# The last two layer visits of a two-block transformer kernel: linear heads' output products behind the first scores, pieces of gate and output products behind the transposes

## The reference

```
h = rmsnorm(x); z = h @ w_in              # linear heads q,k,v, gates, low-rank c, rope key
o_gla = rmsnorm(gla_mix(q, k, v, log_a)) * silu(g_gate)       # linear attention, 4 heads, chunks of 64
q = rmsnorm(c_q) @ w_uq;  kv = rmsnorm(c_kv) @ w_ukv;  head norms and rope
o_mla = block_causal_attention(q, k, v) * silu(m_gate)        # 4 softmax heads of 128
x = x + concat([o_gla, o_mla]) @ w_out[l]
```

## Time and profile before

| | us |
|---|---|
| three runs of the kernel | 1118.04, 1120.25, 1122.82 |
| median | 1120.25 |
| the profiled execution | 1117.79 |
| its span, first to last instruction | 1115.9 |
| TensorE busy in the span | 981.8 (88%) |
| VectorE, ScalarE, GpSimd busy | 657.9, 325.7, 526.7 |
| mean granted TensorE clock | 0.963 of full speed |

### The profile page before, as it was taken

How to read it: one execution, slowest core, us unless ns; L and a number is a source line. 1 busy time by engine, 2 the same in 40 slices (tenths; PEclk the granted TensorE clock), 3 DMA queues, 4 the chain that set the end, 5 groups by cost and what they waited for, 6 DMA issues and landing times.

```text
span 1115.9 us, 11288 instructions
## 1 busy us (share of the span) xinstructions
PE 981.8 (88%) x3307; PEld 530.3 (48%) x3307; DVE 657.9 (59%) x1547; ACT 325.7 (29%) x816; POOL 526.7 (47%) x578
## 2 busy tenths in 40 slices
PE   3999999999997787887769989889899987998997
PEld 3858655864543332332325534434453532554653
DVE  5867776885864865865675576477445554242142
ACT  4113322222221211121143625313363430262251
POOL 1210011767777777777667645656564562100000
PEclk9999999999999899899989999989899988999999
DMA  9998855999999999999999999999999998955750
GB/s 343 318 385 328 313 198 176 378 376 406 409 409 411 411 413 412 411 414 408 400 412 408 410 407 406 403 410 398 411 411 407 405 372 316 396 222 170 258 195 19
DMA packets 142042, 394.92 MB, mean 354 GB/s; under 512 B 16745, under 2 KB 23457, under 8 KB 141857
## 3 DMA queue, kind: packets, MB, share of 16 engines
q0 software_dynamic: 75392, 274.86, 62.6%
q1 hardware_dynamic: 64224, 118.61, 29.3%
q10 hardware_dynamic: 2368, 0.76, 0.3%
HBM read 393.15 MB, written 1.05 MB: 353 GB/s over the span
## 4 chain that ended last, share of the span: by engine, by line
PE 55%; DMA 24%; POOL 8%; issue 6%; DVE 4%; ACT 2%; POOLq 0%; SPq 0%; DVEq 0%; ACTq 0%
PE bank L1755 18%; DMA wring<-in_peer_u,ids 14%; PE bank L1803 13%; PE bank L1489 7%; POOL wring L993 5%; DMA R<-in_w_in 4%; DMA wring<-in_ada_w 3%; PE bank L1824 3%; PE bank L1566 2%; DMA wring<-in_peer_v,ids 2%; POOL R L993 2%; PE bank L1479 1%; DVE wring L2367 1%; PE bank L1850 1%; DMA last_row<-in_peer_v,ids 1%
## 5 line engine op out<-in xcount | busy, mean ns | idle before, releaser
L2367 DVE CUSTOM_DVE_ANT_0 wring<-wring,bank 128x1024 f32<-128x1024 f32 x224 | 273.0, 1219 | 223.3 <-DMA wring<-in_peer_u,ids 220.9
L993 POOL DMA_INDIRECT wring<-in_peer_v,ids x224 | 216.3, 966 | 163.9 <-PE bank L1755 73.0
L1755 PE MATMUL bank<-wring,R 128*128 128x512 f32 x496 | 242.7, 634 | 45.8 <-ACT R L1247 32.9
L993 POOL DMA_INDIRECT wring<-in_peer_u,ids x224 | 212.6, 949 | 76.0 <-issue 57.3
L1755 PE MATMUL bank<-wring,modb 128*128 128x512 f32 x384 | 183.8, 619 | 26.3 <-ACT modb L1247 13.4
L1755 PEld LDWEIGHTS bank<-wring,R 128*128 128x128 f32 x496 | 96.8, 202 | 173.1 <-issue 141.7
L1755 PEld LDWEIGHTS bank<-wring,modb 128*128 128x128 f32 x384 | 71.8, 196 | 116.1 <-issue 89.8
L1032 POOL TENSOR_SCALAR small<-small 128x1 f32<-128x1 f32 (+3 forms) x13 | 2.5, 193 | 218.2 <-ACTq L1328 125.1
L1803 PE MATMUL bank<-R,hT 128*128 128x512 f32 (+1 forms) x192 | 90.4, 599 | 7.1 <-DMA R<-in_w_in 7.1
L1803 PE MATMUL bank<-wring,hT 128*128 128x512 f32 (+1 forms) x192 | 86.4, 600 | 4.3 <-ACT hT L1428 2.7
L1489 PE MATMUL bank<-hT,wring 128*128 128x256 f32 x304 | 70.9, 392 | 2.5 <-DVE hT L2050 1.0
(11 more groups left out here) (387 smaller groups left out, 1269.8 us busy)
## 6 DMA issues: line engine op xcount, KB each, us to landing
wring<-in_w_in SPq DMA_DIRECT2D x14, 2048.0 KB, 12.9
wring<-in_ada_w SPq DMA_DIRECT2D x8, 2048.0 KB, 13.7
R<-in_w_in SPq DMA_DIRECT2D x8, 2048.0 KB, 19.6
wring<-in_w_out SPq DMA_DIRECT2D x6, 2048.0 KB, 10.8
wring<-in_ada_w SPq DMA_DIRECT2D x8, 1024.0 KB, 15.3
R<-in_w_out SPq DMA_DIRECT2D x4, 2048.0 KB, 19.7
wring<-in_peer_wq SPq DMA_DIRECT2D x2, 2048.0 KB, 10.2
wring<-in_peer_u,ids POOLq DMA_INDIRECT x224, 12.4
```

The costliest lines, as they stand in the source:

```text
L993: pool.indirect_dma_start(dst, None, table, bass.IndirectOffsetOnAxis(index, 0)).then_inc(landed, 16)
L1755: last = pe.matmul(pb[half][:, :], diag[b][:, s, :], v_place(n, b, s)[:, half * 512:(half + 1) * 512], start=False, stop=last_row, skip_gr ...
L2367: dve.tensor_tensor_reduce(row, row, h_psum(t), 1.0, 0.0, ALU.mult, ALU.add, a8[:, b, s:s + 1]).then_inc(u_free, 1)
```

## The change

Only the list of `tail_schedule()` is another. Everything that is computed stays, with the same instructions.

```
-    out = [("y2", 1, 0, p) for p in range(4)]
+    out = []
...
-            out += [("y2", 1, 1, p) for p in range(4)]
+        ch = v - LAYERS
+        out += [("y2", 1, ch, p) for p in range(3)]
         to(("zT",), ("zTe",))
-        out.append(("y2e", 1, v - LAYERS))
+        out += [("y2", 1, ch, 3), ("y2e", 1, ch)]
...
-        to(("U",), ("st",), ("ms", 0), ("mk", 0), ("mk", 1), ("mx", 0), ("mx", 1), ("ms", 1), ("mk", 2), ("mg", 2), ("mk", 3))
-        to(("mPT", 0), ("mPTe", 0), ("mPT", 1), ("mPTe", 1), ("mx", 2), ("mx", 3), ("go",), ("gosq",), ("rms", 3))
-        to(("mPV", 0), ("mPV", 1), ("mg", 3), ("mge",), ("mPT", 2), ("mPTe", 2), ("mPT", 3), ("mPTe", 3), ("goe",))
-        to(("mPV", 2), ("mPV", 3), ("moe",), ("cT2", 0), ("cT2e", 0))
-        to(*[("y2", ch, p) for ch in range(2) for p in range(2)], ("cT2", 1), ("cT2e", 1))
+        to(("U",), ("st",), ("ms", 0), ("mk", 0), ("mk", 1), ("mx", 0), ("mx", 1), ("go",), ("gosq",), ("rms", 3), ("ms", 1), ("mk", 2), ("mk", 3))
+        to(("mPT", 0), ("mPTe", 0), ("mPT", 1), ("mPTe", 1), ("mx", 2), ("mx", 3), ("goe",), ("mPV", 0), ("mPV", 1))
+        to(("mPT", 2), ("mPTe", 2), ("mPT", 3), ("mPTe", 3), ("mg", 2), ("mPV", 2), ("mPV", 3), ("cT2", 0), ("cT2e", 0))
+        to(("mg", 3), ("mge",), ("moe",), ("y2", 0, 0), ("y2", 0, 1), ("y2", 1, 0), ("cT2", 1), ("cT2e", 1), ("y2", 1, 1))
```

## The result

| | us |
|---|---|
| changed kernel, median of five | 1113.11 (1111.15 to 1113.55) |
| kernel before, median of five | 1120.07 (1118.04 to 1122.82) |
| ratio of the two, 95% interval | 0.9932 (0.9913 to 0.9952) |
| profiled execution of the changed kernel, its span | 1113.40, 1111.6 |

The change makes the kernel 7.0 us faster; 6.1 was predicted. By the interval it is between 5.4 and 9.7. Profile against profile the gain is only 4.4 us (1117.79 to 1113.40), and when both kernels were measured again (the first experiment) their medians were 5.3 us apart. Where the differences lie is the question of the experiments.

A forecast was written before the change was run, and what follows sets the result against it. From 950 us on TensorE's work bounds the kernel, so closing its holes saves time: 2 x 2.6 + 0.8 - 0.7 + 1.7 - 0.85 = 6.1 us, 1120.25 to 1114.1. Its own range was 1111 to 1117; 1110.5 to 1118.5 with two rivals.

The forecast's parts named there:

- Inside a visit: From the first scores' end to the last output piece: 29.43 us becomes 26.8, 2.6 saved per visit, 5.2 for both.
- the linear output: TensorE product moved to the start of the count, ahead of the second scores, priced at 1.84 us without a wait.
- The wait that the change opens: Behind the first transposes TensorE waits for VectorE's masks and copy: 1.7 us per visit, bounds 1.4 to 2.1.
- No slack at the third value product: Copy behind the linear heads allows it at 9.34 us, TensorE arrives at 9.35; without the covering gate piece 1.7 open.
- The starts of the visits: Moving one output piece behind the normed transposes loses 0.7 us in visit 2 and saves 0.8 in visit 3.
- The clock: Visit 2's half-clock stretch goes, 1.7 us gained; a possible new one at its start costs 0.85, between 0 and 1.7.
- the other case: If transposes counted as a busy TensorE for the clock, the summed gain would be nearer 7.0 us than 6.1.
- the old hole of 2.9 us: Mid-visit stretch of waits and one transpose group before the change; the clock fell behind it in visit 2, not 3.
- 3.75 us for four product rows: Rows after an idle 3.50 us, read as some 1.9 above four at full clock, 1.72.
- Half the gain: Rival: copies and the product behind the linear heads come later, 1.3 us lost a visit; gain 3.5, 1116.8 us; chance 0.14.
- the clock eats it: Rival: full-price slow stretch at visit 2's start and one left in a visit; gain 3.6, 1116.6 us; chance 0.14.
- slower: Rival: linear heads reach VectorE too late for a late root, holes over 3 us; +4.1, 1124.4 us; chance 0.06.

The follow-up runs named there:

- the first experiment: The changed kernel measured again against the kernel before, also called the second comparison: 1113.16 us against 1118.48, ratio 0.9946.
- the cover gone: Changed kernel with the moved gate piece taken from ahead of the third value product and set beside the last gate piece: 1116.30 us, ratio 0.9968.
- the starts alone: Kernel before with only the left-open output piece moved behind the normed transposes: median 1123.07 us in twelve runs, ratio 1.0025; once more, 1123.22.
- the inside alone: Changed kernel with all four left-open output pieces ahead of the normed transposes again, keeping only the new order inside visits: 1112.71 us, ratio 0.9949.
- four pieces ahead: Changed kernel with all four left-open output pieces ahead of the transposes in visit 2, three still in visit 3: 1111.31 us, ratio 0.9931.
- the first copies ahead: Changed kernel with the mask of head 3 moved behind the copies of heads 0 and 1: 1111.61 us, ratio 0.9929.

## Why the prediction was right, and where it was off

**Inside a visit: right, 0.2 short.** Predicted 2.6 us, measured 29.43 - 26.99 = 2.44. The term that was off most is the linear output, 2.04 (1083.42 - 1081.38) instead of 1.84; what makes it longer behind the first scores than behind transposes was not tested. Two heads times values take 1.16 instead of 1.09. The wait that the change opens was predicted at 1.7; it is 1.5 to 1.6, since the second scores end at about 1085.5, the transposes take 0.44 and the product starts at 1087.53 (the profile gives it as 1.40 of idle time, with the transposes' end modelled later). The place (the copy behind the last mask) and the release by VectorE are as predicted.

**No slack at the third value product: right.** Predicted 9.34 and 9.35; in the trace the product starts at 1090.87, 9.49 on that count, with the gate piece ending 0.02 before. With the cover gone the hole was 1.74, predicted 1.7.

**The starts of the visits: the waits right, one term 0.2 short.** In visit 2 0.7 is lost, as predicted. In visit 3 the gain is 1.0, not 0.8: from the transposes to the end of `c` before it is 1047.82 - 1039.69 = 8.13 us, after it 1045.95 - 1037.13 = 8.82, of which the moved piece is 1.72. The prediction counted the copy's wait alone; `c` itself also takes 6.23 instead of 6.46 us when it follows another product without a wait (7.95 less the piece's 1.72). So the starts give 0.3 together, as the kernels with one part alone show: the starts alone 0.3 under the kernel before, the inside alone 0.3 over the changed kernel, four pieces ahead 1.0 under the inside alone, all at full clock (152.7, 148.19 and 147.16 us of tail).

**The clock: the places right, the sizes and one premise off.** For the start of visit 2 I took half of 1.7. The full 1.7 was paid in five of the six profiled executions that have the longer wait there (the changed kernel twice, the cover gone, the first copies ahead, the starts alone once of twice), and in none of the six whose wait stayed at 0.6. The rule of the Trainium skill, page "TensorE: Matmul & The Clock Gate", section "Part 4: PE-mode transpose", that a transpose does not count as a busy TensorE, gave the better number for the profiled pair (5.3 against 5.2 measured in the tail); the runs do not show it by themselves, since no kernel had the transposes away. The 7.0 that the prediction had for the other case equals the difference of the medians, but by luck: it puts the price at the start of visit 2 at nothing, and the full 1.7 was paid. For visit 2 I took away 1.7, from one profile; two more profiles of the kernel before show 2.9 and 3.0, and the kernel with the starts alone shows that it can fall in both visits. That the shorter waits of the new order keep the clock up is true mostly, not always: behind the old hole of 2.9 us it fell in five of ten visits, behind the new one, 2.0 us on the same count and 1.40 of it idle, in one of ten (visit 2 with the cover gone; never in the changed kernel's four). These are few cases, and what decides in a single one stays open.

One reading of the prediction is wrong without bearing on the sum: 3.75 us for four product rows is 2.0 above 1.72, not 1.9.

So of the gain 5.2 is from holes (153.05 us of tail at full clock before, 149.56 - 1.7 = 147.9 after; predicted 5.3). What remains of the median's 7.0 is argued and not shown: two of three profiles of before gave back 2.9 to 3.0 in visit 2 where 1.7 is now paid at the start, which makes 6.4, inside the interval of 5.4 to 9.7. The 7.0 is itself partly chance: its median of the kernel before, 1120.07, stands above the 1118.48 and 1118.17 of the later comparisons, and the second comparison gives 5.3 by medians and 6.0 by its ratio. That 6.1 lies between is in part luck: against those two profiles both of its terms for the clock were too small, the 1.7 given back and the 0.85 paid, and the two errors work against each other. How often the clock falls in executions without a profile stays open, and the profiled executions begin their tails up to 3.2 us apart (957.89 to 961.12), for causes that were not followed.

**The rivals.** "Half the gain" and "slower" needed a later copy or a later root; both were on time. Of "the clock eats it" the first half came true, the slow stretch at the start, and not the second, one left in a visit.

## What to carry to other kernels

When every hole of the leading engine has another engine's name, lay out both engines' lists on one time line and put independent work of the right length into each hole, one piece per hole; a piece that stands where the engine waits for something else anyway (the start of visit 2) costs nothing there, and taking it away cost 0.7 us of waiting and in most profiles 1.7 of clock. A hole in matmul work is worth its length plus what the clock takes behind it, and that second part must be read from several profiles, since one execution shows it at one price or not at all. If the engine that is waited for has too much in its list at that point, reordering it mostly moves the hole (1.40 became 0.64 and 0.47); more cover closed it.

## What the runs showed of the hardware

Behind the same hole of 2.9 us in the old order a half-clock stretch cost 0, 1.7, 2.9 or 3.0 us; it stood there in five of ten visits. The new hole, 1.40 us idle behind four transposes, was followed by such a stretch in one of ten. The kernel whose twelve times fell into two groups, 6 to 7 us apart, gave one profile in each range, and the two differ by 7.6 us in the tail, all of it clock. An idle time of 2.34 us followed by eight transposes was followed by a fall in five of six profiles; an idle time of 0.62 with the same transposes in none of six.
